# Turning the first head pair's queries and keys with VectorE block transposes and transfers in a one-core hybrid decoder layer

## The reference

```python
u = _rmsnorm(x, mix_norm[l]) @ w_in[l]
q1, q2, k1, k2, dv, sq, sk, sv = [u[..., c[i]:c[i + 1]] for i in range(8)]
def prep(t, g):                                   # 4 heads of 128
    t = t.reshape(b, s, DIFF_HEADS, DIFF_QK_DIM)
    return _partial_rope(_rmsnorm(t, g), cos, sin)
q1, q2 = prep(q1, q_norm[l]), prep(q2, q_norm[l])
k1, k2 = prep(k1, k_norm[l]), prep(k2, k_norm[l])
...
w = _softmax_map(q1, k1, mask, t0, t1) - lam * _softmax_map(q2, k2, mask, t0, t1)
outs.append(jnp.einsum('bhqk,bkhd->bqhd', w, vf[:, :t1]))
...
a_out = _rmsnorm(a_out, subln[l]) * (1.0 - lambda_init)
b_out = _stick_breaking(sq, sk, sv).reshape(b, s, SB_WIDTH).astype(x.dtype)
x = x + jnp.concatenate([a_out, b_out], axis=-1) @ w_out[l]
```

## Time and profile before

| | |
|---|---|
| median of 3 runs | 1847.5 us (1847.01 to 1847.59) |
| the profiled execution's own time | 1846.8 us |
| its span in the trace | 1845.0 us |
| TensorE busy | 1835.0 us, 99% of the span |
| VectorE, ScalarE busy | 56%, 45% |
| the mixing stage, first 24 chunks | about 731 to 871 us of the span |

### The profile page before, as it was taken

One profiled execution on the slowest core, in us unless ns is written; L12 is line 12 of the kernel. 1 busy time (PEld: TensorE's weight loads), 2 busy tenths in 40 slices (PEclk: granted clock), 3 DMA queues, 4 the chain that ended last, 5 costly groups with the idle time before them and its releaser, 6 DMA issues.

```text
span 1845.0 us, 21846 instructions
## 1 busy us (share of the span) xinstructions
PE 1835.0 (99%) x8464; PEld 1530.6 (83%) x8464; DVE 1033.9 (56%) x1153; ACT 834.8 (45%) x1064; POOL 15.8 (1%) x19
## 2 busy tenths in 40 slices
PE   9999999999999999999999999999999999999998
PEld 7888888888888888888888888888888888888887
DVE  7555554545444558666666566555544545554565
ACT  7444333444333435564666445343434444333444
POOL 0000000000000000100000000000000000000000
PEclk9999999999999999999999999999999999999999
DMA  9666655566566646655554466665655666566653
GB/s 328 203 205 204 204 195 189 196 197 226 194 198 201 211 152 225 218 175 171 168 187 160 160 216 226 196 212 198 210 187 190 197 199 234 182 232 221 198 170 116
DMA packets 231997, 366.84 MB, mean 199 GB/s; under 512 B 14448, under 2 KB 93040, under 8 KB 231920
## 3 DMA queue, kind: packets, MB, share of 16 engines
q1 hardware_dynamic: 230432, 363.91, 59.6%
q10 hardware_dynamic: 1488, 1.87, 0.3%
HBM read 346.85 MB, written 2.10 MB: 189 GB/s over the span
## 4 chain that ended last, share of the span: by engine, by line
PE 99%; DVE 0%; DMA 0%; POOL 0%; ACT 0%; DVEq 0%; issue 0%; SPq 0%
PE psum L1625 86%; PE psum L1526 7%; PE psum L1531 3%; PE psum L1645 1%; PE psum L1747 0%; PE psum L1758 0%; PE psum L1793 0%; PE psum L1773 0%; DVE x_res L1477 0%; DMA w_raw<-in_ffn_gate 0%; PE psum L1493 0%; PE psum L1491 0%; PE psum L1492 0%; PE psum L1559 0%; PE psum L1806 0%; PE psum L1757 0%
## 5 line engine op out<-in xcount | busy, mean ns | idle before, releaser
L956 DVE TENSOR_TENSOR w_split<-w_raw,w_split 128x1024 fp32r<-128x1024 f32 (+1 forms) x660 | 769.9, 1208 | 624.0 <-ACT w_split L558 622.4
L1625 PE MATMUL psum<-w_split,x_split 128*128 128x512 f32 x4752 | 1083.4, 390 | 0.0
L558 ACT ACTIVATE w_split<-w_raw 128x1024 fp32r<-128x1024 f32 (+1 forms) x660 | 656.3, 1042 | 915.1 <-PE psum L1625 873.4
L1625 PEld LDWEIGHTS psum<-w_split,x_split 128*128 128x128 f32 x4752 | 891.2, 188 | 185.2 <-DVE w_split L956 0.6
L1625 PE MATMUL psum<-w_split,h_split 128*128 128x512 f32 x2208 | 502.2, 389 | 0.0
L1625 PEld LDWEIGHTS psum<-w_split,h_split 128*128 128x128 f32 x2208 | 414.3, 188 | 85.9
L1526 PE MATMUL psum<-x_split,w_split 128*128 128x512 f32 x256 | 79.9, 396 | 0.0
L1108 DVE SCALAR_TENSOR_TENSOR strip_sum<-psum,rstd_tok,normed 128x512 f32<-128x512 f32 x44 | 31.0, 747 | 45.2 <-PE psum L1625 45.2
L1531 PEld LDWEIGHTS psum<-x_split,w_split 128*128 128x128 f32 x256 | 46.9, 188 | 10.6
L1526 PE MATMUL psum<-h_split,w_split 128*128 128x512 f32 x168 | 51.8, 395 | 0.0
L1531 PE MATMUL psum<-x_split,w_split 128*128 128x256 f32 x256 | 49.1, 278 | 0.0
(11 more groups left out here) (185 smaller groups left out, 547.7 us busy)
## 6 DMA issues: line engine op xcount, KB each, us to landing
w_raw<-in_ffn_up SPq DMA_DIRECT2D x87, 1024.0 KB, 5.4
w_raw<-in_ffn_gate SPq DMA_DIRECT2D x86, 1024.0 KB, 5.2
w_raw<-in_ffn_down SPq DMA_DIRECT2D x76, 1024.0 KB, 5.1
w_raw<-in_w_in SPq DMA_DIRECT2D x48, 512.0 KB, 4.8
w_raw<-in_w_in SPq DMA_DIRECT2D x24, 1024.0 KB, 5.1
w_raw<-in_w_out SPq DMA_DIRECT2D x16, 1024.0 KB, 5.2
lo_sum<-head_out SPq DMA_DIRECT2D x480, 32.0 KB, 1.9
w_raw<-in_ffn_down SPq DMA_DIRECT2D x16, 768.0 KB, 4.7
```

What stands on the lines that cost most here:

```text
L558: nc.scalar.activation(w_split[:, slot % 2, 0, h * half:(h + 1) * half], w_raw[:, slot, h * half:(h + 1) * half], ACT.Copy).then_inc(hi_ma ...
L956: nc.vector.tensor_tensor(w_split[:, slot % 2, 1, part], w_raw[:, slot, part], w_split[:, slot % 2, 0, part].bitcast(F32), ALU.subtract).t ...
L1625: ins = mm(psum[:, bank + t, :], x[:, a, t * P:(t + 1) * P], w[:, b, k, :], start=kk == 0 and (a, b) == (0, 0), stop=kk == count - 1 and a ...
```

## The change

The pieces of the first pair (n = 0 to 3) are no longer turned on TensorE: the table has `qk_turn` for n = 4 to 7 only. When VectorE has scaled pieces 1 and 3, it makes two block transposes of the pair of pieces into `turned_32`; SP moves them with 16 transfers after the load of chunk 9 and again after that of chunk 13 into `hidden_moved`; ScalarE reads them from there with their gain in four instructions a time (`moved_qk_gain`), at chunks 7 and 11 of its list. `scores` of the first pair stands after chunk 12 instead of 10, `lambda` after 13, `turn` after 18 instead of 15, `values` after 19 instead of 16, and what hangs on them in the lists goes along. Since `hidden_moved` is taken, the output of both pairs moves through `normed`; the first pair's goes after the load of chunk 26, waits for all turned pieces of the second pair (`qk_turned`, 4), and is read at chunk 26.

```diff
     for n, m in enumerate(qk_strip):
-        pe_steps.append((2 * (m | 1) + 3, "qk_turn", n))
-    pe_steps.append((11, "lambda", 0))
+        if n >= 4:
+            pe_steps.append((2 * (m | 1) + 3, "qk_turn", n))
+    pe_steps.append((13, "lambda", 0))
     for p in range(2):
-        pe_steps += [(12 * p + 10, "scores", p), (12 * p + 15, "turn", p), (12 * p + 16, "values", p)]
+        late = 2 * (p == 0)
+        pe_steps += [(12 * p + 10 + late, "scores", p), (12 * p + 15 + late + late // 2, "turn", p), (12 * p + 16 + late + late // 2, "values", p)]
...
-    out_moves = {23: 0, 35: 1}
-    out_read_at = {22: 0, 37: 1}
+    qk_moves = {9: 0, 13: 1}
+    qk_read_at = {7: 0, 11: 1}
+    out_moves = {26: 0, 35: 1}
+    out_read_at = {26: 0, 37: 1}
...
+                def move_qk(pair):
+
+                    sp.wait_ge(qk_32, pair + 1)
+                    for q in range(4):
+                        for a in range(4):
+                            sp.dma_start(hidden_moved[32 * q:32 * q + 32, a, :, :, :], turned_32[32 * a:32 * a + 32, q, :, :, :]).then_inc(
+                                qk_landed, 16)
...
                     sp.wait_ge(out_32, p + 1)
+                    sp.wait_ge(qk_turned, 4)
...
+                def moved_qk_gain(pair):
+                    act.wait_ge(qk_landed, 256 * (pair + 1))
+                    for n in (2 * pair, 2 * pair + 1):
+                        kind = n // 2
+                        for t in range(2):
+                            ins = nc.scalar.activation(qk[:, n, :, t * P:(t + 1) * P].rearrange("p h (a j) -> p h a j", a=4),
+                                                       hidden_moved[:, :, 2 * (n % 2):2 * (n % 2) + 2, t, :].rearrange("p a h j -> p h a j"),
+                                                       ACT.Copy, scale=rest_gain[:, kind:kind + 1])
+                        ins.then_inc(qk_ready, 1)
...
-                    if n > 1:
-                        dve.wait_ge(qk_turned, n - 1)
-                    nc.vector.tensor_tensor(normed[:, n % 2, :, :].rearrange("p b (h d) -> p b h d", h=2), by_head(j),
+                    if n > 5:
+                        dve.wait_ge(qk_turned, n - 5)
+                    nc.vector.tensor_tensor(normed[:, :, n % 2, :].rearrange("p b (h d) -> p b h d", h=2), by_head(j),
...
+                    if n in (1, 3):
+                        dve.wait_ge(qk_normed, n + 1)
+                        for t in range(2):
+                            ins = nc.vector.transpose(turned_32[:, :, :, t, :].rearrange("p q b j -> p b q j"),
+                                                      silu_out[:, t, :].rearrange("p (b q j) -> p b q j", b=4, q=4))
+                        ins.then_inc(qk_32, 1)
...
-                    if kind == "qk_turn":
-                        after[cc - 2].append((qk_rope, n))
-                        early[cc - 1].append((qk_means, n))
-                        after[cc - 1].append((qk_normalize, n))
...
+                for n, m in enumerate(qk_strip):
+                    after[2 * (m | 1) + 1].append((qk_rope, n))
+                    early[2 * (m | 1) + 2].append((qk_means, n))
+                    after[2 * (m | 1) + 2].append((qk_normalize, n))
```

More of the change, by code:

```diff
@@ L206, in hybrid_layer @@
         out_tok = qk[:, 2:4, :, :].rearrange("p a b n -> p (a b n)")
-        out_moved = [hidden_moved, normed[:, :, :, :].rearrange("p a b n -> p (a b n)").rearrange("p (a b t j) -> p a b t j", a=4, b=4, t=2)]
+        out_moved = normed[:, :, :, :].rearrange("p a b n -> p (a b n)").rearrange("p (a b t j) -> p a b t j", a=4, b=4, t=2)
         hidden_tok = strip_sum[:, :, :, :].rearrange("p t a n -> p t (a n)")
@@ L316, in hybrid_layer @@
         out_normed = sem("out_normed")
+        qk_32 = sem("qk_32")
+        qk_landed = sem("qk_landed")
         out_32 = sem("out_32")
@@ L466, in four_chunks @@
                             sp.dma_start(dst, source(i, j)).then_inc(landed[j], 16)
+                        if ph["kind"] == "mix" and c - 2 * ph["s0"] in qk_moves:
+                            move_qk(qk_moves[c - 2 * ph["s0"]])
                         if ph["kind"] == "mix" and c - 2 * ph["s0"] in out_moves:
@@ L804, in evict_first @@
                     ins.then_inc(lo_copied, 2)
+                def moved_qk_gain(pair):
[7 more added lines that the diff above has]
+                        ins.then_inc(qk_ready, 1)
                 def qk_gain(n):
-                    act.wait_ge(qk_turned, n + 1)
+                    act.wait_ge(qk_turned, n - 3)
                     kind = (n % 4) // 2
@@ L854, in out_hi_parts @@
                             ins = nc.scalar.activation(h_split[:, 2 * p:2 * p + 2, d, 0, t * P:(t + 1) * P].rearrange("p h (a j) -> p h a j", a=4),
[L855 removed]
+                                                       out_moved[:, :, d:4:2, t, :].rearrange("p a h j -> p h a j"), ACT.Copy,
                                                        scale=subln_gain[:, d:d + 1])
@@ L895, in mix @@
                         after[cc].append((sb_hi_parts, n))
+                for cc, pair in qk_read_at.items():
+                    after[cc].append((moved_qk_gain, pair))
                 for cc, p in out_read_at.items():
@@ L1343, in out_lo_parts @@
                                 high, low = (h_split[:, 2 * p + h, d, n, t * P:(t + 1) * P].rearrange("p (a j) -> p a j", a=4) for n in range(2))
-                                ins = stt(low, out_moved[p][:, :, 2 * h + d, t, :], subln_gain[:, d:d + 1], high.bitcast(F32),
+                                ins = stt(low, out_moved[:, :, 2 * h + d, t, :], subln_gain[:, d:d + 1], high.bitcast(F32),
                                           ALU.mult, ALU.subtract)
@@ L1746, in qk_turn @@
                         at = h * T + b * P
-                        ins = nc.tensor.transpose(psum[:, qk_bank(n), at:at + P], normed[:, n % 2, b, h * P:(h + 1) * P],
+                        ins = nc.tensor.transpose(psum[:, qk_bank(n), at:at + P], normed[:, b, n % 2, h * P:(h + 1) * P],
                                                   const("ident"))
```

2 lines of the change are left out of this document (1 added, 1 removed).

## The result

The changed kernel takes **1850.2 us** (median of 22 runs, 1848.99 to 1851.52), the kernel before beside it 1847.2 us (22 runs, 1846.55 to 1848.07). The ratio is 1.0016, with a 95% interval of 1.001 to 1.0022: slower by 3.0 us, by an amount just inside the 0.2% that the prediction called the limit. The profiled execution took 1849.16 us with a span of 1847.4 us, against 1846.8 and 1845.0 before.

The account below looks back on a forecast made before the run. TensorE bounds the kernel without slack, so late steps cost in full: -1.74 for the turns, +2.9 and +1.9 for two waits, sum +3.1 us on a median of 1847.5, giving 1850.6 us; range 1847.5 to 1853.5.

Parts of the forecast that it names:

- The turns gone: TensorE after chunks 5 and 9: two turns of eight transposes, 0.87 us each, leave the path, -1.74 us.
- Moves, reading and scores covered: Block transposes, SP's two moves and ScalarE's reading before the scores after chunk 12 cost nothing; slack 0.6 to 1.0 us.
- Rival C: After chunk 12 the scores wait 0.7 to 1.5 us for the second move: 1851.3 to 1852.1 us, chance 0.08.
- signs of being wrong: Among them, a wait for a load of weights after one of SP's moves, excluded with 4 us of slack.
- The first wait: After chunk 17, TensorE waits 2.9 us for VectorE's scaling of pieces 4 and 5, behind late second exponentials.
- GpSimd's powers: Before the turn of pieces 4 and 5: the pair ends at 828.7, covered by the split of chunk 18 until 829.45.
- The second wait: After chunk 21, TensorE waits 1.9 us for the scaling of pieces 6 and 7, behind the output's scaling and transposes.
- sign of being right: TensorE's turns wait twice for `normed`: 2 to 3.5 us, then 1.5 to 2.5 us.
- Rival A: At the turns after chunks 17 and 21, one wait is missing (chance 0.08) or both (0.07): 1845.8 to 1848.7 us.
- rival B: In the gap before the turn of pieces 4 and 5 the clock falls, costing 2.7 us: 1853.3 us, chance 0.15.
- the likeliest case: Both waits at the turns after chunks 17 and 21, clock kept: 1849.8 to 1851.6 us, chance 0.60.

Follow-up runs that it names:

- Both scalings in front: Changed kernel with VectorE's scaling of pieces 4 and 5 ahead of inverses and weights, and of 6 and 7 ahead of the first pair's output normalization: 1845.89 us.
- second set of 10 runs: The changed kernel, unedited, timed again beside the kernel with added matmuls: 1849.58 us, ratio 1.0016 to the kernel before.
- the filled gap: Changed kernel plus eight matmuls with unused result on TensorE between chunk 17 and its wait for scaled pieces 4 and 5: 1849.42 us, ratio 1.0012.
- pieces 6 and 7 in front: Changed kernel with VectorE's scaling of pieces 6 and 7 ahead of the first pair's output normalization, which goes to other memory: 1849.33 us, ratio 1.001.
- first pair turned on TensorE: Changed kernel without the first pair's block transposes and moves, turned on TensorE after chunks 5 and 9; later scores and VectorE order kept: 1851.44 us.
- the earlier scores: Changed kernel with the first pair's scores after chunk 11 and lambda after 12, one chunk sooner: 1857.74 us, ratio 1.0057.
- rope and means in front: Changed kernel with rope and means of pieces 4 and 5 ahead of the inverses on VectorE, scaling still behind the weights: 1848.67 us, ratio 1.001.
- pieces 4 and 5 in front: Changed kernel with rope of pieces 4 and 5 ahead of the inverses and their scaling ahead of the weights on VectorE: 1847.22 us, ratio 1.000.
- the scaling ahead of the weights: Changed kernel with only the scaling of pieces 4 and 5 ahead of the first pair's weights on VectorE: 1850.10 us, ratio 1.0016.

## Why the prediction was right, and where its sum was off

The forecast was 1850.6 us, and 1850.2 was measured. Its steps:

- **The turns gone, -1.74 us: right.** Both scalings in front give 1845.9 us, 1.2 us under before. With 0.23 us more in the first turn 1.5 us was to be expected. In the stage itself the trace has it in full: from the last step ahead of it (730.28 and 730.61) to the start of chunk 24 (871.22 and 869.97) it is 140.94 us before and 139.36 with both in front, 1.58 less. The two profiled spans differ by only 0.8 us (1845.0 and 1844.2): 0.33 us of the rest lies ahead of the stage and 0.45 behind it, where TensorE does the same work in both; what it is, I have not found.
- **Moves, reading and scores covered: right, to 0.3 us.** SP's moves were forecast at 761.5 to 771.6 and 784.4 to 794.4, and stand at 761.64 to 771.9 and 784.54 to 794.56. The slack ahead of the scores is 0.9 us (forecast 0.6 to 1.0). Rival C did not happen. One of the signs of being wrong did show, on ScalarE: the rounding of chunk 14 waits 1.97 us for its load behind the second move and starts at 799.92, where the load was forecast for 799.3. TensorE doesn't feel it, as the prediction had it.
- **The first wait: mechanism right, size 0.4 us too large.** Exponentials done 824.95 (forecast 825.0), `normed` in the forecast's place. Two errors of size: TensorE starts on piece 4 as soon as it alone is scaled, at 831.2, and not when both are, at 831.8; and the chain through inverses, rope, split and weights ran 0.4 us shorter than its sum (scaling at 830.54 for 830.9). The wait is 2.11 us, and the turn then runs with the scaling of piece 5 and takes 1.26 instead of 1.03. Net 2.49 instead of 2.9.
- **GpSimd's powers "covered by the split": wrong reasoning, without effect here.** I took 1.98 us for the pair from the earlier trace rows, where VectorE had nothing to do beside it, and had it end at 828.7. It took 3.55 us and ended at 830.17, 0.4 us ahead of the scaling. It does bind as soon as the weights are moved away.
- **The second wait: mechanism right, size 1.63 instead of 1.9**, for the same reason: the turn starts when piece 6 is scaled. The wait in the list is 1.24 us, under the 1.5 to 2.5 us that the prediction gave as a sign of being right; most of the rest of the 1.63 us is in the turn, which takes 1.26 us instead of 1.03 beside the scaling of piece 7.
- **Rival A, a wait missing: false; rival B, the clock: by the times, true in about half of the runs.** The prediction set it beside the forecast with a chance of 0.15 and a price of 2.7 us, as something that happens or doesn't, and had it decide the outcome as soon as it happens. It happens in one execution and not in the next, at a price of 1.6 us. In the 22 runs of the changed kernel 8 lie below 1849.5 us and 11 at 1850.48 or above; the median falls between.

So that the forecast's 1850.6 comes within 0.4 us is partly luck, two errors that cancel: the two waits were 0.7 us too large together (4.8 for 4.12), and the clock was left out of the likeliest case. In the median it is worth 0.6 us by the sum of the terms (3.0 less 2.38) and 0.9 by the lower group: without a fall of the clock the kernel takes about 1849.3 us. In the second set of 10 runs, with 4 in the upper group, the median is 1849.58. That the upper group of the changed kernel's own runs are falls of the clock is inferred: by the size (1.6 us), by the gap in the same place in the two kernels whose profile shows the fall, and by the filled gap. Neither of the two profiled executions of the changed kernel itself has one; both (1849.16 and 1849.29) are of the lower group. In the main set of runs the mean granted clock is 0.998 in the 8 below 1849.5 us and 0.997 or 0.996 in the 14 above, which agrees, but weakly, as 0.997 is also found in kernels without such a gap.

## What to carry to other kernels

Where one engine is on the path without a break, an instruction taken off it is only a gain if the lists of the other engines still put first what that engine needs next; here the same instructions in another order are worth some 4 us, more than twice what the turned pieces were. When a step is moved to another chunk, follow each list it appears in to its new neighbours, and ask of each consumer what stands ahead of it now; the first to be late hides a second, which shows as soon as the first is mended. And a short operation priced from a row where its neighbour was idle may take twice as long beside a busy one.

## What the runs showed of the hardware that I had not expected

**The clock can fall after a gap of 2.1 us, and need not.** With gaps of 2.10 us (pieces 6 and 7 in front) and 2.10 us (first pair turned on TensorE), TensorE busy up to the gap, the granted clock went to 0.50 (1.2 GHz) some 0.6 and 1.0 us after the turn had begun, and came back about 3.4 us later; with 2.11 and 2.10 us (both profiles of the changed kernel) it stayed at 1.00. With the earlier scores it fell behind the 4.41 us gap, and once more behind gaps of 1.37 and 0.94 us with four transposes between them. Each fall at the turn of pieces 4 and 5 cost 1.6 us. Why one execution has it and the next not, the traces do not show. The Trainium skill (TensorE: Matmul & The Clock Gate, "HAM oscillation — how this bites in real kernels") says that idle gaps between matmuls throttle TensorE again and that it loses half of the time spent throttled; the traces agree on the price, with 1.6 us lost for some 3.4 us at half clock, and show the fall in two of the four profiled executions with the 2.1 us gap.

**Two tiny powers on GpSimd take 1.98 to 4.15 us, by what VectorE does.** On 128x4 elements each, the pair took 1.98 us with VectorE nearly idle (and 1.98 again with rope and means in front), 2.42 us with pieces 4 and 5 in front, 3.55 us in the changed kernel, and 4.15 us in two others, all but the 1.98 beside VectorE's split of a chunk, two instructions of 1.21 us each. The first power takes 1.01 us in all of them; only the second is stretched. With both scalings in front:

```profile
825.94 2.41 POOL L535 TENSOR_TENSOR head_rstd<-head_mean,const_sb 128x4 f32<-128x4 f32 x2 [46.37 <-DVE head_mean L1297]
```

```profile
826.27 2.35 DVE L985 TENSOR_TENSOR w_split<-w_raw,w_split 128x1024 fp32r<-128x1024 f32 x2
```

The second power ends 0.87 us after the end of one of VectorE's instructions each time: here (828.35) after the first half of the split (826.27 + 1.21 = 827.48); in the changed kernel (830.17) after the second half (826.95 + 2.35 = 829.30); with the scaling ahead of the weights (830.90) after the scaling of piece 4, which follows the split there (829.35 + 0.68 = 830.03). So it looks as if the power waited for one, two or three of them and then ran. The Trainium skill (SBUF — State Buffer, "Who interferes with whom") says that a VectorE instruction with two SBUF inputs and a GpSimd instruction that reads SBUF exclude each other, the later one blocking until the first has finished. The split and the scaling have two such inputs, and the ends agree. No run here varied the operands, so this cause is argued, not shown, and why the power gets in behind the first half in one order and not in the other stays open. The profile's spans on GpSimd are rough, but the long ones are real: VectorE waited 0.90 us for the second power in both kernels with 4.15.
